# Preparing the next heads at a fixed rate in a two-layer diffusion trunk, with sixteen adaLN pieces and one input block moved

## The reference

```
for i in range(2):
    sh1, sc1, g1, sh2, sc2, g2 = split(silu(cond) @ ada_w[i] + ada_b[i], 6)      # adaLN terms
    h = rms_norm(x, g_mix) * (1 + sc1) + sh1
    if i == 0:                                    # pooling mixer beside latent attention
        u, cq, ckv, krope = split(h @ w_in)       # widths 512, 384, 256, 32
        y_pool = (windowed mean of u - u, windows 2, 4, 8, 16) @ w_pool * scale
        q = rope(rms_norm(rms_norm(cq) @ w_uq))                    # 8 heads of 96
        k, v = split(rms_norm(ckv) @ w_ukv); k = rope(rms_norm([k, krope]))
        # latent tokens also see 512 cached context tokens (cache_ckv, cache_krope)
        y = [y_pool, softmax(q @ k.T / sqrt(96)) @ v] @ w_out
    else:                                         # chunked spatial gating
        u, v = split(h @ w_in); y = (u * (w_s @ rms_norm(v) + b_s)) @ w_out
    x = x + g1 * y
    h = rms_norm(x, g_ffn) * (1 + sc2) + sh2
    x = x + g2 * ((silu(h @ wg) * (h @ wu)) @ wd)
```

## Time and profile before

| | |
|---|---|
| median of 3 runs | 1259.85 us (1257.9 to 1291.38) |
| the profiled execution | 1259.46 us; its span on the slowest core, core 5: 1258.4 us |
| spans of the 8 cores | 1248.7 to 1258.4 us |
| PE busy in the span | 1137.0 us (90%), 6857 matmuls |
| DVE, ACT, POOL busy | 480.3 us (38%), 429.5 us (34%), 227.8 us (18%) |
| moved by the DMA queues | 90.04 MB; read from memory 153.85 MB, since weights are stored as float32 |
| chain that ended last | PE 76%, DVE 7%, DMA 6%, ACT 5%, POOL 3% |

### The profile page before, as it was taken

How to read it: one execution, slowest core, us unless ns; L and a number is a source line. 1 busy time by engine, 2 the same in 40 slices (tenths; PEclk the granted TensorE clock), 3 DMA queues, 4 the chain that set the end, 5 groups by cost and what they waited for, 6 DMA issues and landing times.

```text
span 1258.4 us, 17871 instructions; the slowest of 8 cores (1248.7 to 1258.4 us)
## 1 busy us (share of the span) xinstructions
PE 1137.0 (90%) x6857; PEld 547.9 (44%) x6857; DVE 480.3 (38%) x814; ACT 429.5 (34%) x669; POOL 227.8 (18%) x347
## 2 busy tenths in 40 slices
PE   2477678797889899999999999998899999999998
PEld 1233455554544344444444444444344444444443
DVE  0355673634136211152252253565622225125133
ACT  2455466665745511101101156543651110110100
POOL 3311452533213200000000022224310000000000
PEclk9988997868799899999999999998999999999999
DMA  9960318778991425225224206003533321410013
GB/s 187 239 110 1 59 30 141 112 118 130 155 167 36 67 38 92 39 35 84 34 34 84 51 1 109 1 1 49 98 55 67 68 35 34 84 17 1 1 76 126
DMA packets 24977, 90.04 MB, mean 72 GB/s; under 512 B 3392, under 2 KB 3776, under 8 KB 24128
## 3 DMA queue, kind: packets, MB, share of 16 engines
q0 software_dynamic: 21312, 77.10, 36.8%
q1 hardware_dynamic: 3584, 11.80, 2.8%
HBM read 153.85 MB, written 6.88 MB: 128 GB/s over the span
## 4 chain that ended last, share of the span: by engine, by line
PE 76%; DVE 7%; DMA 6%; ACT 5%; POOL 3%; issue 3%; POOLq 0%; ACTq 0%; DVEq 0%
PE pb L230 74%; DMA wslot<-w_in_u 3%; DMA wslot<-ada_w 3%; ACT pt L247 2%; DVE xtmp L268 2%; PE pb L228 2%; DVE kT L274 1%; POOL qs L251 1%; DVE xb L268 1%; DVE qf L274 1%; POOL qr L251 1%; ACT hy L247 0%; ACT xsq L247 0%; POOL qt L251 0%; DVE utok L251 0%
## 5 line engine op out<-in xcount | busy, mean ns | idle before, releaser
L230 PE MATMUL pb<-hb,wslotx 128*128 128x512 bf16 x1440 | 319.9, 379 | 0.0
L247 ACT ACTIVATE sg<-pb 128x512 f32<-128x512 f32 x132 | 78.7, 596 | 472.0 <-PE pb L230 472.0
L251 DVE TENSOR_TENSOR apart<-pb,sg 128x512 bf16<-128x512 f32 x132 | 91.3, 691 | 369.0 <-PE pb L230 346.2
L230 PEld LDWEIGHTS pb<-hb,wslotx 128*128 128x128 bf16 x1440 | 140.8, 98 | 170.0 <-issue 0.3
L268 DVE SCALAR_TENSOR_TENSOR xb<-pb,mod,xb 128x512 f32<-128x512 f32 x192 | 143.6, 749 | 143.1 <-PE pb L230 143.1
L230 PE MATMUL pb<-hb,wslot 128*128 128x512 bf16 x864 | 197.6, 385 | 0.0
L230 PE MATMUL pb<-apart,wslot 128*128 128x512 bf16 x768 | 167.1, 379 | 0.0
L247 ACT ACTIVATE pt<-pb,rk 128x1024 bf16<-128x1024 f32 (+1 forms) x128 | 118.9, 953 | 58.0 <-PE pb L230 57.2
L230 PEld LDWEIGHTS pb<-hb,wslot 128*128 128x128 bf16 x864 | 85.6, 99 | 104.9 <-issue 5.7
L230 PEld LDWEIGHTS pb<-apart,wslot 128*128 128x128 bf16 x768 | 75.1, 98 | 90.2
L230 PE MATMUL pb<-hy,wslot 128*128 128x512 bf16 (+1 forms) x336 | 82.4, 397 | 4.7 <-ACT hy L247 4.5
(11 more groups left out here) (130 smaller groups left out, 953.8 us busy)
## 6 DMA issues: line engine op xcount, KB each, us to landing
wslot<-ada_w POOLq DMA_DIRECT2D x48, 512.0 KB, 10.1
wslot<-ffn_wd POOLq DMA_DIRECT2D x16, 512.0 KB, 9.9
wslotx<-ffn_wu POOLq DMA_DIRECT2D x14, 512.0 KB, 10.6
wslotx<-ffn_wg POOLq DMA_DIRECT2D x12, 512.0 KB, 18.9
y<-xb SPq DMA_DIRECT2D x12, 512.0 KB, 2.7
wslot<-ffn_wg POOLq DMA_DIRECT2D x10, 512.0 KB, 7.4
xb<-x_in POOLq DMA_DIRECT2D x4, 1024.0 KB, 41.7
wslot<-ffn_wu POOLq DMA_DIRECT2D x8, 512.0 KB, 7.5
```

What stands on the lines that cost most here:

```text
L230: return self.op("pe", lambda g: g.matmul(out, lhsT, rhs, start=start, stop=stop), [lhsT, rhs], [out], inc=inc)
L247: return self.op("act", lambda g: g.activation(out=out, in_=in_, func=func, bias=bias, scale=scale), reads, [out])
L251: return self.op(e, lambda g: g.tensor_tensor(out=out, in0=in0, in1=in1, op=op), [in0, in1], [out])
```

## The change

The edits, in the order of the program:

- Eleven slots at the start in place of ten (still three of them retired), and seven in place of eight added after attention. `in_q1` is so issued ahead of x block 1.
- x block 2 is issued behind the third adaLN piece, so behind `in_u0`, `in_u1` and piece 8.
- Pieces 8 to 19 stand ahead of `ukv`, `uq0`, `uq1` in the list. Pieces 9 to 13 are so issued ahead of the constants.
- The projection's fillers have fixed rates (`together`): of the next norm 24 steps over the ten stops, in block 1 nine steps of pooling and five adaLN pieces, in block 2 seven pieces. The pieces use bank 6.
- `qkv` has units of q, k and v in turn. Pair 0 is prepared with one step of pooling at each stop (bank 6 alone) and up to four pieces (bank 7).
- In attention, 18 stops of `qkv` are spread over 25 steps, and the remaining pieces evenly over the 108.
- The third norm scale tile is shared with the first, `ckr_f` is dropped early, and `new` takes the smallest gap that fits.

```
-        addr = gaps[-1][1] - nbytes if high else gaps[0][0]
+        addr = gaps[-1][1] - nbytes if high else min(gaps, key=lambda g: (g[1] - g[0], g[0]))[0]
...
-        slots = [new("wslot%d" % i, [128, 2048], BF16, high=(i >= 7)) for i in range(10)]
+        slots = [new("wslot%d" % i, [128, 2048], BF16, high=(i >= 8)) for i in range(11)]
...
-        ent("ukv", w_ukv, 2, 1024)
+        ent_ada(8, 20)
         ent("uq0", w_uq[:, 0:2, :], 2, 768)
         ent("uq1", w_uq[:, 2:3, :], 1, 768)
-        ent_ada(8, 48)
+        ent("ukv", w_ukv, 2, 1024)
+        ent_ada(20, 48)
...
-        W.retire.update((7, 8, 9))
+        W.retire.update((8, 9, 10))
...
-                self.rs = [new("xrs%d" % i, [128, 512], F32) for i in range(3)]
+                self.rs = [new("xrs%d" % i, [128, 512], F32) for i in range(2)]
+                self.rs.append(self.rs[0])
...
         for k in range(8):
             ada_piece()
-            if k == 1:
+            if k == 2:
                 load_x("pool", 2)
...
+        def ada_gen():
+            k0 = ada_state["done"]
+            for k in range(k0, 50):
+                if k - 2 >= k0:
+                    W.done(("ada", k - 2))
+                if k < 48:
+                    ada_piece(pool=AB, keep=True)
+                yield 0.4
+
+        AB = (6,)
+        ada = ada_gen()
+
+        def together(main, n, parts):
+            for i, _ in enumerate(main):
+                for g, k in parts:
+                    for _ in range((i + 1) * k // n - i * k // n):
+                        next(g, None)
 
         for b in range(3):
             drain(norms[b])
-            fill = collections.deque()
+            parts = []
             if b < 2:
-                fill.append(norms[b + 1])
+                parts.append((norms[b + 1], 24))
+            if b == 1:
+                parts.append((pooling([0], (6,), 0, lambda o, i, sc: P.ts("dve", o, i, sc, None, ALU.mult)), 9))
             if b > 0:
-                fill.append(pooling([b - 1] if b == 1 else [], (6,), 1.3, lambda o, i, sc: P.ts("dve", o, i, sc, None, ALU.mult)))
-            weave_in(inproj(b), fill)
+                parts.append((ada, 5 if b == 1 else 7))
+            together(inproj(b), 10, parts)
...
+            order = [("q", 0, 0), ("k", 3), ("q", 0, 1), ("v", 3), ("q", 1, 0), ("k", 0), ("q", 1, 1), ("v", 0),
+                     ("q", 2, 0), ("k", 1), ("q", 2, 1), ("v", 1), ("k", 2), ("v", 2)]
+            for kind, *arg in order:
+                {"q": q_unit, "k": k_unit, "v": v_unit}[kind](*arg)
                 yield 0.5
                 tick()
...
-        q0 = qkv(0, (0, 1, 2, 3, 4, 5))
-        weave(q0, collections.deque([pooling([1, 2], FB, 0.5, lambda o, i, sc: P.act(o, i, AF.Copy, scale=sc))]), flush=True)
+        pool12 = pooling([1, 2], (6,), 0, lambda o, i, sc: P.act(o, i, AF.Copy, scale=sc))
+        AB = (7,)
+        together(qkv(0, (0, 1, 2, 3, 4, 5)), 18, [(pool12, 18), (ada, 4)])
+        drain(pool12)
+        AB = FB
...
-        debt = 0.0
-        for i, idle in enumerate(attention(before)):
-            debt += idle
-            while debt > 0:
-                t = next(nxt[0], None)
-                if t is None:
-                    debt = 0.0
-                    break
-                debt -= t
-            if i % 5 in (1, 3):
+        left = 50 - ada_state["done"]
+        for i, _ in enumerate(attention(before)):
+            n = i % 28
+            for k in range((n + 1) * 18 // 25 - n * 18 // 25):
+                next(nxt[0], None)
+            if (i + 1) * left // 108 > i * left // 108:
                 next(ada, None)
```

More of the change, by code:

```diff
@@ L825, in build @@
         key_sums(3)
+        drop(ckr_f)
         def inproj(b):
@@ L979, in build @@
         N.close()
-        drop(*sqb.t, *rsb.t, *t2k.t, sqkr, ckr_f, ropek, *held)
+        drop(*sqb.t, *rsb.t, *t2k.t, sqkr, ropek, *held)
         wukv = W.get("ukv")
@@ L1051, in reduce @@
                 P.op("dve", lambda g: g.reduce_sum(out=ss[:, 4 * u:4 * u + 4], in_=qs[:], axis=AX.X), [qs[:]], [ss[:, 4 * u:4 * u + 4]])
[L1053 to L1075, removed]
@@ new lines, in q_unit @@
+            def q_unit(b, u):
+                if u == 0:
+                    qst[b] = (ssr.next(), ssr.next(), [])
+                ss, sr, qts = qst[b]
+                ps = P.bank(banks)
+                for i in range(2):
+                    t = 4 * b + 2 * u + i
+                    P.mmg(ps[:, i * 192:(i + 1) * 192], [(cqn[:, kc, t * 128:(t + 1) * 128], wuq[kc][:, p * 192:(p + 1) * 192]) for kc in range(3)])
+                qf = qfr.next()
+                qs = qsr.next()
+                qt = qtr.next()
+                qts.append((qf, qt))
+                P.cp("dve", qf[:].rearrange("p a d -> p (a d)"), ps[:, 0:384])
+                P.tt("pool", qs[:], qf[:], qf[:], ALU.mult)
+                later(1, functools.partial(reduce, ss, u, qs))
+                if u == 1:
+                    later(2, functools.partial(rnorm, ss, sr))
+                    for v in range(2):
+                        later(3 + v, functools.partial(rotate, b, v, qts[v][0], qts[v][1], sr))
+                    later(6, functools.partial(turn, b, [x[1] for x in qts]))
@@ L1086, in sums, with k_unit @@
                 P.tt("dve", ksb[:, kb * 4:kb * 4 + 4, :], ps[:, 0:8].rearrange("p (a b) -> p a b", b=2), k_bc, ALU.add)
-            for kb in (3, 0, 1, 2):
+            def k_unit(kb):
                 ps = P.bank(banks)
-                lw = [wukv[:, kc, p * 256:p * 256 + 128] for kc in range(2)]
-                P.mmg(ps[:], [(lw[kc], ckvn[kb][:, kc, :]) for kc in range(2)])
+                P.mmg(ps[:], [(wukv[:, kc, p * 256:p * 256 + 128], ckvn[kb][:, kc, :]) for kc in range(2)])
                 sq = sqk.next()
@@ L1095, in qkv, with v_unit, krstd @@
                     P.cp("act" if p == 0 and hl == 1 else "dve", kT[0:64, hl, blk(kb)], ps[hl * 64:hl * 64 + 64, :])
-                yield 0.43
-                tick()
+                later(2, functools.partial(sums, kb, sq))
+            def v_unit(kb):
                 ps = P.bank(banks)
                 for i in range(4):
-                    rv = [wukv[:, kc, p * 256 + 128:p * 256 + 256] for kc in range(2)]
-                    P.mmg(ps[:, i * 128:(i + 1) * 128], [(ckvn[kb][:, kc, i * 128:(i + 1) * 128], rv[kc]) for kc in range(2)])
+                    P.mmg(ps[:, i * 128:(i + 1) * 128],
+                          [(ckvn[kb][:, kc, i * 128:(i + 1) * 128], wukv[:, kc, p * 256 + 128:p * 256 + 256]) for kc in range(2)])
                 P.cp("dve", V[:, kb * 4:kb * 4 + 4, :, 0:64], ps[:].rearrange("p (t h d) -> p t h d", t=4, h=2))
+            def krstd():
+                P.act(ksb[:], ksb[:], AF.Ln, bias=epsc[:, 3:4])
+                P.act(rk[:], ksb[:], AF.Exp, scale=-0.5)
+                drop(ksb)
+            qst = {}
+            order = [("q", 0, 0), ("k", 3), ("q", 0, 1), ("v", 3), ("q", 1, 0), ("k", 0), ("q", 1, 1), ("v", 0),
+                     ("q", 2, 0), ("k", 1), ("q", 2, 1), ("v", 1), ("k", 2), ("v", 2)]
+            for kind, *arg in order:
+                {"q": q_unit, "k": k_unit, "v": v_unit}[kind](*arg)
                 yield 0.5
                 tick()
[L1105 to L1112, removed]
+            later(2, krstd)
             while lag:
@@ L1115, in qkv @@
                 tick()
[L1117 to L1124, removed]
         SD = [P.pb[:, 0:1024], P.pb[:, 1024:2048]]
@@ L1241, in build @@
         N = Norm()
-        W.more([new("wslotx%d" % i, [128, 2048], BF16) for i in range(8)])
+        W.more([new("wslotx%d" % i, [128, 2048], BF16) for i in range(7)])
         norms = {}
@@ L1253, in build @@
         drop(*hy)
-        W.more([new("wslotx%d" % i, [128, 2048], BF16) for i in range(8, 8)])
+        W.more([new("wslotx%d" % i, [128, 2048], BF16) for i in range(7, 7)])
         stage(ffn(0, need(0, 1)), fill, norms, 1, 0, hbs)
```

21 lines of the change are left out of this document (3 added, 18 removed).

## The result

The changed kernel takes 1269.0 us (median of 7 runs), the kernel before 1258.95 on the same chip: a ratio of 1.0086, 95% interval 1.006 to 1.0111. It is slower by about 0.9%; the forecast was 1249, or 0.8% faster, so the time lies inside the range but on the other side of no change.

A forecast was written before the change was run, and what follows sets the result against it. PE was taken to bound the projection; in attention no engine was full, ACT idling for want of scores. 1259.5 + 15.2 (projection) + 0 (pair 0) - 25.5 (attention) = 1249 us, range 1229 to 1271.

The forecast's parts named there:

- pair 0: Preparation before attention: better unit order against one pooling bank, three added pieces and late `ukv`; 0, between -5 and +4 us.
- The projection: Three blocks ahead of the first pair's preparation: 15.2 us later in sum, between +6 and +21.
- `band` and the low clock behind it: Block 1: `band` lands at 93 behind added pieces, 7.3 us later net, plus 3.4 us of low clock.
- block 0's gain: First projection block: second u weight lands sooner, so the block ends some 6 us sooner.
- pieces in block 1 and bank 6: Block 1: five pieces cost PE 2.8 us; four wait for VectorE to read the bank, 4.8 us.
- the norm at a fixed rate: Blocks 1 and 2: norm done earlier removes a wait and low clock; -7 us, at best -8.4, other end -3.
- seven pieces in block 2: Block 2: pieces keep PE busy 3.9 us more, with no bank wait.
- Attention: Four pairs: fewer pieces and spread filler save 8 us in each of three, 1.5 in the last; -25.5, between -8 and -45.
- the price of the spacing: Filled attention pairs: spreading filler saves 5 us each, a third of ACT's idle 15.0 us.
- the second: Rival, chance 0.18: in attention a fill costs the same wherever it stands, only pieces' 8 us return; 1268 us.
- Rival 1: Attention falls to its exponentials: filled pairs 39 us, the last 34, -41 in all; 1231 us, chance 0.20.
- rival 3: Projection: added pieces do not hold `band` back, their loads taking 4.3 us, not 9.7; 1244 us, chance 0.07.
- rival 4: Both stretches go wrong: 20 us in projection, a loss in pair 0, nothing from attention; 1285 and above, chance 0.04.

The follow-up runs named there:

- three edits: Changed kernel with band and pw loaded ahead of x block 2, no adaLN pieces in block 1, and pair 0's pooling in two banks: 1240.4 us, ratio 0.9838.
- all in attention: Changed kernel with all 42 piece stops in attention, band and pw loaded ahead of x block 2, pair 0's pooling in two banks: 1244.97 us, ratio 0.9874.
- old rate: The three edits kernel, units in the new order but prepared by the credit of before instead of the even rate: 1266.83 us, ratio 1.0029.
- attention part alone: Kernel before with only the new `qkv` order and the even-rate attention loop, nothing moved ahead of attention: 1261.6 us, ratio 0.9997.

## Why the prediction was wrong

The step that failed first is pair 0, taken "at 0, between -5 and +4": it cost 6.9 us. The price was in the text, "pooling has one bank in place of two", and was set off against a gain of the order that the trace never showed. The one bank is 3.5 us of it (35.3 to 31.8). The three pieces are 1.1 (31.5 against 30.4, three edits against all in attention), and the new order at fixed stops 2.0 (30.4 against 28.4, all in attention against before); both are within what the same code differs by between executions, and why the last is there stays open.

The projection was forecast at +15.2 within +6 to +21; `qf` starts 20.8 us later (median 138.6 to 159.4). Its terms:
- `band` and the low clock behind it, 7.3 + 3.4 = 10.7 with block 0's gain taken off: measured 10.9 - 1.2 = 9.7. Right in sum. But block 0 ended 1.2 us sooner and not 6, because the normed block 1 was the next thing late (2.76 us at 79.98); the wait for `band` was 7.8 us and not 14, since it began later.
- pieces in block 1 and bank 6, 2.8 + 4.8 = 7.6: measured 13.0. This is the mis-sized term. The wait was priced by one copy of 1.2 us, while VectorE's queue held `cqn` and the norm applications, which the same change had moved in among the band steps: the four waits behind a band step are 9.6 us and not 4.8, and a fifth of 2.9 had no price.
- the norm at a fixed rate, -7: measured -4.2 (2.3 in block 1, 1.9 in block 2, before against all in attention, with `band`'s old wait in it).
- seven pieces in block 2, 3.9: measured 2.4 (19.8 to 22.2).

Together 9.7 + 13.0 - 4.2 + 2.4 = 20.9.

Attention, -25.5 forecast, gave 22.2 on the median core: 7.2 by the fifteen pieces that left (173.0 to 165.8; forecast 8.1), 15.0 by the rest (188.0 to 173.0; forecast 17.4). The size held, the reason lacked a part: the slot was "taken at nothing", and without it the 15.0 are 2.5. Nor is the gain mainly less waiting, from which the forecast took the price of the spacing: of the 22.2 us PE's waits are 3.2 (34.7 to 31.5) and its busy time 17.2 (150.3 to 133.1), of which fifteen pieces of 0.55 us make 8.2; the other 9 come with a clock of 0.92 over attention in place of 0.85, for which the sum had 3 x 0.8 us.

Against the forecast the projection is 5.6 us longer, pair 0 6.9, and attention gives back 3.3 less: 15.8 together, which turns a gain of 10 into a loss. On the median core the sum is 20.8 + 6.9 - 22.2, with 1.9 less after attention: +3.6 where spans show +4.6 (1256.0 to 1260.6; medians don't add up exactly). The rest belongs to the slowest core. Before, it was 2.4 us above the median core, after it 6.2. On core 1 this comes from attention, 172.2 us against a median of 165.8, with the clock of 0.62 in its last pair; but core 7 is only 1.2 us shorter than core 1, and it lost 3.5 us before pair 0 began (`qf` at 162.9). The forecast was made on one core and had no term for this spread.

Of the rivals, the second gave 1268, close to what came, by a mechanism that the runs refute: attention returned more than the 15 us from which it was to decide, and the old rate shows that spacing matters. Rival 1 is refuted by pairs of 43.4 us, rival 3 by `band` at 92, rival 4 by attention. Of the signs that were to show the prediction wrong neither came (`band` by 85, a filled pair at 50 or below 40): no sign watched pair 0 or the waits for bank 6, where the loss was.

## What to carry to other kernels

A wait for a bank is priced by all that stands ahead of the eviction in its engine's queue, and a change that moves work onto that engine raises the price of every such wait. A load that is queued behind weights for later use was late here by their whole transfer time, whoever uses them: look at the order of issue first. When a stall is removed, ask what is late next: here even spacing was worth nothing until one more buffer kept the weights on time, and the buffer nothing without the spacing.

## What the hardware showed unexpectedly

TensorE's granted clock over attention (medians) was 0.83 in the attention part alone, 0.87 with all pieces in attention and the slot, 0.92 in the changed kernel with fifteen pieces fewer, and 0.82 at the old rate. The sum of PE's waits doesn't explain it: 32.0, 26.8, 31.5 and 41.5 us in the same order. What raises the clock stays open. And single cores of one execution differ by 6.1 us in the last pair, 32.4 us at 1.00 and 38.5 at 0.61, with the same matmuls; the slowest of eight cores passes this on to the whole.
